# Attention in slots: later turns, copies and gathers of the weights, and a fifth buffer of turned weights

## What is computed

```
logits = einsum('bqhd,bkhd->bhqk', qi, k) * scale          # a block of 128 queries
mask = key_pos[None, :] < q_pos[:, None]
log_beta = log_sigmoid(logits)
log_1m_beta = where(mask, log_sigmoid(-logits), 0.0)
after = cumsum(log_1m_beta, axis=3, reverse=True) - log_1m_beta
w = where(mask, exp(log_beta + after), 0.0)
out = einsum('bhqk,bkhd->bqhd', w, v)
```

## Time and profile before

| | us |
|---|---|
| median of 3 runs | 2953.42 |
| lowest and highest | 2952.36, 2954.19 |
| the profiled execution | 2953.14 |
| its span in the trace | 2951.4 |
| the attention in it, first score to last y | 608.5 to 1098.4 |

### The profile page before, as it was taken

One profiled execution on the slowest core, in us unless ns is written; L12 is line 12 of the kernel. 1 busy time (PEld: TensorE's weight loads), 2 busy tenths in 40 slices (PEclk: granted clock), 3 DMA queues, 4 the chain that ended last, 5 costly groups with the idle time before them and its releaser, 6 DMA issues. The chain is left out here.

```text
span 2951.4 us, 42837 instructions
## 1 busy us (share of the span) xinstructions
PE 2726.0 (92%) x14883; PEld 2246.9 (76%) x14883; DVE 1839.1 (62%) x2733; ACT 1346.5 (46%) x2268; POOL 903.1 (31%) x711
## 2 busy tenths in 40 slices
PE   6999977879989879996999899999999999999998
PEld 5888864757777767885888688887888787878787
DVE  5344338957877776555667765656556748485753
ACT  4222224657777764323444455555554424242421
POOL 0011101645655542120000032333333334444442
PEclk9999988989999999997999999999999999999999
DMA  5433344282222205523222344334544465647554
GB/s 172 106 81 90 86 135 67 65 219 61 72 62 55 80 10 157 142 85 135 93 86 100 111 136 132 102 102 149 171 131 133 129 156 100 167 104 169 99 113 86
DMA packets 291138, 328.19 MB, mean 111 GB/s; under 512 B 113816, under 2 KB 220320, under 8 KB 290720
## 3 DMA queue, kind: packets, MB, share of 16 engines
q1 hardware_dynamic: 276704, 291.96, 33.3%
q0 software_dynamic: 13824, 33.56, 7.7%
q10 hardware_dynamic: 464, 0.79, 0.1%
HBM read 206.57 MB, written 126.88 MB: 113 GB/s over the span
## 5 line engine op out<-in xcount | busy, mean ns | idle before, releaser
L3256 PE MATMUL f_ps_bank<-f_big,h_wv 128*128 128x512 f32 x1280 | 503.3, 393 | 25.4 <-DVE f_big L3102 15.9
L3257 PE MATMUL f_ps_bank<-f_big,h_wv 128*128 128x512 f32 x1280 | 500.8, 391 | 0.0
L3258 PE MATMUL f_ps_bank<-f_big,h_wv 128*128 128x512 f32 x1280 | 500.8, 391 | 0.0
L787 DVE TENSOR_TENSOR_SCAN a_left<-a_left,a_ps_one 128x640 f32<-128x640 f32 (+5 forms) x192 | 319.7, 1676 | 45.8 <-ACT a_left L755 45.2
L738 POOL TENSOR_TENSOR a_w<-a_on,a_left 128x640 f32<-128x640 f32 (+5 forms) x192 | 281.9, 1470 | 208.0 <-DVE a_left L787 162.6
L2999 ACT ACTIVATE h_wv<-h_w_sum 128x512 fp32r<-128x512 f32 x252 | 159.0, 631 | 348.9 <-PE f_ps_bank L3258 322.6
L2942 POOL TENSOR_TENSOR h_w_sum<-h_w_raw 128x512 f32<-128x512 f32 x63 | 90.7, 1439 | 734.2 <-DMA h_w_raw<-in_w_up 456.2
L3256 PEld LDWEIGHTS f_ps_bank<-f_big,h_wv 128*128 128x128 f32 x1280 | 241.9, 189 | 83.0 <-issue 26.0
L3258 PEld LDWEIGHTS f_ps_bank<-f_big,h_wv 128*128 128x128 f32 x1280 | 241.9, 189 | 50.7
L3257 PEld LDWEIGHTS f_ps_bank<-f_big,h_wv 128*128 128x128 f32 x1280 | 242.0, 189 | 49.8
L3098 DVE TENSOR_TENSOR h_wv<-h_w_raw,h_wv 128x512 fp32r<-128x512 f32 x189 | 173.3, 917 | 159.6 <-ACT h_wv L2999 156.3
(11 more groups left out here) (400 smaller groups left out, 6015.0 us busy)
## 6 DMA issues: line engine op xcount, KB each, us to landing
h_w_raw<-in_w_up SPq DMA_DIRECT2D x32, 1024.0 KB, 6.8
a<-h_xr SPq DMA_DIRECT2D x128, 256.0 KB, 3.4
h_w_raw<-a SPq DMA_DIRECT2D x32, 1024.0 KB, 5.2
h_raw<-in_w_down SPq DMA_DIRECT2D x32, 512.0 KB, 6.6
out<-h_xr POOLq DMA_DIRECT2D x64, 256.0 KB, 4.8
out<-h_xr POOLq DMA_DIRECT2D x32, 512.0 KB, 5.6
p_xt<-in_x SPq DMA_DIRECT2D x16, 512.0 KB, 4.6
q<-p_raw SPq DMA_DIRECT2D x64, 128.0 KB, 2.5
```

The lines of the kernel that those rows point to most:

```text
L787: dve.tensor_tensor_scan(part, part, one[:, 0:1].to_broadcast([P, k1 - k0]), 1.0 if first else left[a][i % 2][:, at + k1:at + k1 + 1], ALU ...
L3256: pe.matmul(o, wv(i, 0)[:, k, :], hv(i, 0)[:, k, :], start=(k == 0), stop=False)
L3257: pe.matmul(o, wv(i, 0)[:, k, :], hv(i, 1)[:, k, :], start=False, stop=False)
L3258: mm = pe.matmul(o, wv(i, 1)[:, k, :], hv(i, 0)[:, k, :], start=False, stop=(k == KH - 1))
```

## The change

Four lags and one count of buffers are changed, nothing else. A turn comes three slots behind instead of two, a copy five instead of four, the gather of a pair covers slots m - 7 and m - 6 instead of m - 5 and m - 4, and the copy of y comes eight behind instead of six. `wt` has five buffers of 128 x 1024 instead of four. The buffers of `w` and `on` stay at three each, and the PSUM areas stay as they are.

```diff
@@ -593,8 +593,8 @@
     SLOTS = [(s, a, *u) for s in range(STEPS) for u in UNITS for a in range(2)]
     N = len(SLOTS)
     PER_STEP = N // STEPS
-    ONS, WS, WTS = 3, 3, 4
-    TURN_LAG, COPY_LAG, GATHER_LAG, Y_LAG = 2, 4, 4, 6
+    ONS, WS, WTS = 3, 3, 5
+    TURN_LAG, COPY_LAG, GATHER_LAG, Y_LAG = 3, 5, 6, 8
     with ExitStack() as ctx:
         def sb(name, shape, dt=F32):
             return ctx.enter_context(nc.sbuf_tensor("a_" + name, shape, dt))
```

## The result

The changed kernel takes 2961.35 us (median of 10 runs, 2958.06 to 2964.48) against 2953.36 us of the kernel before (10 runs, 2950.68 to 2955.34): 8.0 us or 0.28% more, a ratio of 1.0028 with a 95% interval of 1.0018 to 1.0038. So by its median it is slower by just over the 0.2% that count as a difference, though the lower end of the interval lies under 0.2%. The forecast of 2957.9 us was 3.4 us too low and named no change that counts; the range held what came.

The account below looks back on a forecast made before the run. PE was taken as attention's main bound, with DVE full in growing slots. The turn's 2 us plus 2.5 us net of delayed work gave +4.5, forecasting 2957.9 us; the range was 2946 to 2972.

Parts of the forecast that it names:

- The bound: PE in attention: busy 438.65 of 492 us, at most 53 us idle to win; 0.63 us gaps at odd turns stay.
- The turn's move: POOL's weighing waits for a later turn, delaying ACT by 0.6 us a pair; 0 to 58 us, taken as 2.
- the ring: Three buffers of w: weighing slot m waits for the turn of slot m - 3, which now comes an iteration later.
- the rival with the chance of 0.34: Slower: ACT's `on` of odd slots waits behind POOL's weighing, as w's three buffers become the bound; +17 us, 2970.4.
- Work put off: PE has one more turn and gather left after each score: 3.07 + 3 x 2.24 = 9.8 us if nothing returns.
- 7.3 that come back: At step starts, the copy of y's 5.5 us wait for a store and the gathers' 1.8 us wait are won back.
- I take both in full: Counts all 9.8 us of delayed PE work and all returned waits: 9.8 - 5.5 - 1.8 = +2.5 us.
- The stretch of growing slots: Where slots grow from 4 to 8 tiles, DVE is full (18.56 of 19.00 us), PE not (16.19); DVE stays over 95%.
- The page's rule: Trainium skill's rule that repeated PE gaps can mean too few buffers; the forecast named the PSUM bank, left at two.
- a rival of 0.03: Faster: PE's gaps come from too few buffers of turned weights and go, taking all 53 us idle; 2900 us, chance 0.03.

Follow-up runs that it names:

- the fastest run: The kernel before with its copies three slots back instead of four and nothing else changed; 2897.24 us, ratio 0.9816.

## Why the prediction was right and where it was wrong

**The bound** was read rightly: PE idle for up to 53 us, in gaps of 0.6 us, ended by a copy that comes late in its engine's order (two iterations behind the turn). Two experiments changed only the distance between turn and copy, from two iterations to one, in the kernel before and in the changed one. PE's idle time in attention fell to 436.0 - 426.70 = 9.3 us in the first, and the time by 55 and 56 us. All runs at distance two lie between 2942 and 2964 us; all at distance one lie between 2897 and 2908, but for the one with its copies between the sigmoids. That the change leaves this distance at two, and so the gaps, was the main point of the forecast, and it held.

**The turn's move** was right in kind: ACT's wait came where and as large as forecast, POOL's rose less than forecast (169.4 us, not over 200). The 2 us that were to reach PE are neither shown nor excluded: taking the ring away with nothing else changed gave 1.7 us, within the noise. It is not the 17 us of the rival with the chance of 0.34, the ring as the bound. That rival named the right sign by the wrong mechanism.

**Work put off** is the term that was mis-sized. It was put at 9.8 us, less 7.3 that come back, +2.5. In attention the change cost 7.1. The step that failed is "I take both in full": the wait for the last store shrank by 5.5 - 4.2 = 1.3 us and not by 5.5, and the wait of the gathers by 1.5. With 2.8 back instead of 7.3 the sum is 9.8 - 2.8 = 7.0. The copy of y did move two slots, but the gather whose result is stored came later too, so the wait moved with it, from 862.18 to 868.51 us. That 7.0 lies beside the 7.1 is in part luck, for the 9.8 does not lie where the prediction put it, as the next numbers show.

The traces tell the parts by place. Behind the last score the kernel before needs 14.7 us (14.7 again with a fourth buffer of w), the gather alone late 17.5, the change 19.3, where some 3 us more were forecast and 4.6 came. Between slot 15 and the last slot, from one start of ACT's `on` (line 751) to the other, it is:

| | us |
|---|---|
| before | 1083.92 - 633.96 = 450.0 |
| before with a fourth buffer of w | 1087.89 - 639.27 = 448.6 |
| the gather alone late | 1084.61 - 634.88 = 449.7 |
| the change | 1088.27 - 636.00 = 452.3 |
| the change with four buffers of turned weights | 1089.24 - 635.18 = 454.1 |
| the changed lags with four buffers of w and of turned weights | 1087.36 - 633.42 = 453.9 |

The first and the last row hold a dip of the granted clock of some 1.7 us, the first that from 742 to 761; the others hold none, so 448.6 is the number to start from. The late gather then costs some 1 us before the last score and 2.8 behind it, though the prediction charged it mostly at the start of each step. The change costs 3.7 before and 4.6 behind. So the later turn and copy cost 2.6 us or more before the last score, and some 2 behind it. These are single executions. The first 16 slots are left out because they took 24 to 30 us in them, with the granted clock at 0.65 to 0.88 in three that were read; that cannot be laid on the change.

Why the third slot of the turn costs this stays open. By the medians the changed lags cost 8.0 us and the gather alone 2.6, so turn and copy together add 5.4. With the distance at one, a turn a slot later adds 2903.72 - 2897.24 = 6.5 us (5.1 when each is taken against its own runs of the kernel before; the intervals overlap), the late gather 1.4 and a fourth slot of lag 2.4, both within the noise. With distance two a fourth slot added nothing. These amounts do not follow the 1.10 and 1.97 us of PE work slot by slot.

**The stretch of growing slots** was read rightly, though "DVE stays over 95%" came out as 88% between 864 and 884 us. Behind the wait at 868.51 us DVE is at 96% again. It is also the part that the fastest run could hardly shorten. In the third step, from the scan of the second slot with four tiles to that of the second with eight, first before, then in the fastest run:

```profile
862.39:878.69 16.30, 14.07 (x117) 10.83 (x118) 16.04 (x17) 13.92 (x22) 10.76 (x8) 1.00 0.05 18
```

```profile
835.53:851.60 16.07, 15.51 (x133) 12.21 (x129) 16.07 (x17) 15.03 (x25) 10.99 (x8) 1.00 0.05 17
```

DVE is busy for 16.04 of 16.30 us and then for all of 16.07. It is the bound there, with or without the gaps. Over the same scans in steps 2 to 4 the fastest run is 3 of its 54 us faster (48.0 against 51.1).

**The page's rule** had a rival of 0.03. The Trainium skill (Perfetto Trace Analysis, Identifying Performance Opportunities) says that consistent bubbles can mean too few buffers in SBUF or PSUM, and to find what the gap waits for and make it start sooner. The trace agrees with the second: no buffer was added in the fastest run (2897.24 us), the same two banks were released one iteration earlier. Fourth and fifth buffers in SBUF changed nothing measurable (0.9999 with a fourth of w); a third bank in PSUM was not tried.

## What to carry to other kernels

When lags are shifted, write down the differences between neighbouring stations; the wait on the short ring of banks was set here by the difference, not by either lag. Find the one wait that ends last before the bound engine, here a bank that is freed by a copy queued behind two sigmoids, and change the number that stands in its chain; moving all stations together left it as it was and only put work off. Then check the other way: a queue may wait for a long time without cost (ACT's 70 us), but the same wait put ahead of an instruction that the bound engine needs cost 128 us (3032.02 against 2903.72).

## What the runs showed of the hardware

A gap costs more than its idle time. With the same 4176 matmul instructions and a mean granted clock of 0.99 in both, PE was busy 438.65 us of attention before and 426.70 us in the fastest run. So of the 54 us won there, 12 are busy time. The pair read shows how, first before, then in the fastest run:

```profile
693.53 0.34 PE L844 MATMUL a_ps_z<-a_k_lo,a_q 128*128 128x384 f32 x1
693.92 0.85 PE L858 MATMUL a_ps_wt<-a_ident,a_w 128*128 128x128 f32 x6
```

```profile
684.59 0.34 PE L844 MATMUL a_ps_z<-a_k_lo,a_q 128*128 128x384 f32 x1
...
684.77 0.82 PE L858 MATMUL a_ps_wt<-a_ident,a_w 128*128 128x128 f32 x6
```

In the fastest run the turn starts at 684.77, 0.16 us before the recorded end of the multiplication ahead of it (684.93); before, it starts 0.05 us behind that end (693.87), and no idle time is listed. So a turn that comes late loses this overlap of 0.16 us on top of the idle time shown. Of the 1.07 us won in this pair 0.21 lie at the first turn and the rest at the second, which had 0.63 us of listed idle time.

The clock at the start of attention is not the same in each execution: 0.88, 0.72 and 0.65 of full speed in the first 20 us of three profiles. With 0.65, slot 15 came 4 us later than with 0.88, and with 0.72 it came 0.9 us later. Four microseconds are half of the change read here, so parts were compared from slot 15 on.
